# Last tokens of two attentions in four column groups, a scan for a suffix sum, and fewer value tiles in a chain of two transformer blocks

## The reference

```python
xn = rms_norm(h, norm_gains[layer, 0])
proj = xn @ w_in[layer]
q_a, k_a, v_a, f_a, q_b, k_b, v_b, g_a, g_b = split(proj)
# forgetting attention, 8 heads of 64, s <= t
s = q_a k_a / 8 + c[t] - c[s]        # c = cumsum(log sigmoid(f_a + b))
o_a = softmax(s) v_a
# stick-breaking attention, 8 heads of 64, s < t
z = q_b k_b / 8
log_keep = log_sigmoid(-z)
later = cumsum(log_keep, reverse) - log_keep
o_b = exp(log_sigmoid(z) + later) v_b
mixed = (sigmoid(g_a) * (o_a @ w_o_fox) + sigmoid(g_b) * (o_b @ w_o_sb)) @ w_out
# end of block 2
h = h + sigmoid(hn @ ple_w_gate) * (p @ ple_w_proj)
out = rms_norm(h, final_norm)
```

## Time and profile before

| | |
|---|---|
| median of 3 runs | 2233.86 us (2232.55 to 2235.23) |
| profiled execution, own time | 2239.25 us |
| profiled execution, span | 2237.4 us |
| mean granted TensorE clock | .989 of full speed |
| busy: PE, DVE, ACT, POOL | 98%, 44%, 33%, 45% |
| chain that ended last | PE 79%, issue 8%, DVE 7%, POOL 4%, ACT 2% |
| DMA | 194.93 MB, mean 87 GB/s |

### The profile page before, as it was taken

One profiled execution on the slowest core, in us unless ns is written; L12 is line 12 of the kernel. 1 busy time (PEld: TensorE's weight loads), 2 busy tenths in 40 slices (PEclk: granted clock), 3 DMA queues, 4 the chain that ended last, 5 costly groups with the idle time before them and its releaser, 6 DMA issues.

```text
span 2237.4 us, 31159 instructions
## 1 busy us (share of the span) xinstructions
PE 2197.2 (98%) x12456; PEld 1888.3 (84%) x12456; DVE 983.5 (44%) x1432; ACT 736.1 (33%) x971; POOL 1001.2 (45%) x800
## 2 busy tenths in 40 slices
PE   8999999989999999999999999999999999999998
PEld 7897988989999887888888887878777888888886
DVE  5134233458988505422200718751776442322027
ACT  4133243432222215322211414553336332222133
POOL 4322211555555547555544544154431554555442
PEclk9999999999999999999999999999999999999998
DMA  4311111222222222422222221013220223222231
GB/s 160 100 63 58 62 47 38 95 76 76 94 94 94 103 94 76 150 94 94 94 96 101 89 107 66 20 62 119 103 94 20 76 94 108 95 97 94 94 118 70
DMA packets 31837, 194.93 MB, mean 87 GB/s; under 512 B 3968, under 2 KB 4480, under 8 KB 9984
## 3 DMA queue, kind: packets, MB, share of 16 engines
q1 hardware_dynamic: 26352, 182.66, 22.9%
q10 hardware_dynamic: 5392, 10.94, 1.5%
HBM read 189.23 MB, written 4.23 MB: 86 GB/s over the span
## 4 chain that ended last, share of the span: by engine, by line
PE 79%; issue 8%; DVE 7%; POOL 4%; ACT 2%; DMA 0%; SPq 0%; DVEq 0%; POOLq 0%; ACTq 0%
PE ps L2104 69%; POOL wlo L617 4%; PE ps L2628 2%; DVE sqa L1365 1%; PE ps L2376 1%; PE ps L2836 1%; PE ps L2753 1%; PE ps L2810 1%; DVE x2lo L1353 1%; PE ps L2726 1%; PE ps L2359 1%; ACT whi L682 0%; PE ps L2791 0%; PE ps L2416 0%; DVE sd L1929 0%
## 5 line engine op out<-in xcount | busy, mean ns | idle before, releaser
L617 POOL TENSOR_TENSOR wlo<-raw,whi 128x512 fp32r<-128x512 f32 (+2 forms) x796 | 1001.0, 1289 | 1207.4 <-ACT whi L682 1117.1
L682 ACT CAST whi<-raw 128x2048 fp32r<-128x2048 f32 x165 | 315.3, 1911 | 826.2 <-PE ps L2104 767.5
L2104 PE MATMUL ps<-x2hi,whi 128*128 128x512 f32 x1136 | 451.3, 397 | 2.3 <-POOL wlo L617 1.2
L2104 PE MATMUL ps<-x2hi,wlo 128*128 128x512 f32 x1136 | 443.3, 390 | 0.0
L2104 PE MATMUL ps<-x2lo,whi 128*128 128x512 f32 x1136 | 443.1, 390 | 0.0
L2104 PE MATMUL ps<-xhi,whi 128*128 128x256 f32 x1344 | 277.9, 289 | 19.0 <-DVE xlo L1418 9.6
L2104 PE MATMUL ps<-xlo,whi 128*128 128x256 f32 x1344 | 274.2, 286 | 0.0
L2104 PE MATMUL ps<-xhi,wlo 128*128 128x256 f32 x1344 | 274.0, 286 | 0.0
L2104 PEld LDWEIGHTS ps<-x2hi,whi 128*128 128x128 f32 x1136 | 214.1, 188 | 52.5 <-issue 7.8
L2104 PEld LDWEIGHTS ps<-x2lo,whi 128*128 128x128 f32 x1136 | 214.0, 188 | 45.3 <-issue 2.6
L2104 PEld LDWEIGHTS ps<-x2hi,wlo 128*128 128x128 f32 x1136 | 213.8, 188 | 44.9
(11 more groups left out here) (399 smaller groups left out, 2779.8 us busy)
## 6 DMA issues: line engine op xcount, KB each, us to landing
raw<-wstream SPq DMA_DIRECT2D x170, 1024.0 KB, 4.8
h<-h SPq DMA_DIRECT2D x4, 528.0 KB, 8.6
ncb<-c_rows ACTq DMA_DIRECT2D x8, 256.0 KB, 3.6
ple_rows<-ple_out ACTq DMA_DIRECT2D x4, 512.0 KB, 4.0
bias<-bias_rows ACTq DMA_DIRECT2D x8, 256.0 KB, 4.5
ple<-ple_rows ACTq DMA_DIRECT2D x4, 512.0 KB, 5.4
out_dram<-outb SPq DMA_DIRECT2D x8, 256.0 KB, 2.9
raw<-wstream ACTq DMA_DIRECT2D x4, 256.0 KB, 7.3
```

The lines of the kernel that those rows point to most:

```text
L617: return nc.gpsimd.tensor_tensor(wlo[b][:, cols], raw[b][:, cols], whi[b][:, cols].bitcast(F32), ALU.subtract)
L682: nc.scalar.copy(whi[b][:], raw[b][:]).then_inc(sig("hi_done"), 1)
L2104: ins = mm(dst, w[slot][:, cols], xx(tok), start=first and p_ == 0, stop=last and p_ == 2, skip_group_check=True)
```

## The change

It does six things.

- The probabilities' turn and the output of both corners are in four column groups (`turn_corner`, `corner_out`): five products per group with the values as the moving side, 128 columns, query-major in 32 rows; `corner_back` turns the 128x128 result after a copy by ScalarE two steps on.
- The stick-breaking corner's scores are query-major in four groups like the fox's. Its suffix sum is a `tensor_tensor_scan` of VectorE backwards over the keys, with ScalarE's exp, ln and exp around it; masks come from a small tile loaded with `fw0`.
- The fifth value tile has, in place of eight k-steps of three matmuls, two calls of `v_tail` (`rows_at` lists j = 4 only for k = 3 and 7): eight matmuls each, the last 32 tokens' activations in float32 (`x_tail`, made by VectorE) with `whi` and with `wlo` in four groups, a k-step each. The four groups' sums stay apart in the fifth block of 128 rows, and the corner's last turned block repeats its 32 keys four times, so that the output's product adds them. `rcol` gets its fifth column from a copy of `rt` repeated four times.
- `V_ORDER` so has 34 items and `T_GATES` and `T_END` are 98 and 226; `tiles_by(step)` is max(8 x step - 6, 5 x step), so steps 0 and 1 have five tiles and all others of fox eight, of which a QKB chunk's last is the sixth.
- Which chunks VectorE evacuates and which units ScalarE casts in a step follows from `tiles_by`, so both shift.
- At the end of block 2 ScalarE scales the result of seven of the eight chunks, the last weight unit is cast one gate earlier, its low parts come in pieces of 128 columns that TensorE waits for quarter by quarter, and the turns are in another order.

The diff, cut to its core:

```diff
@@ -436,18 +442,19 @@
-        V_FIRST = [(j, k) for js in ((0, 1, 2), (3, 4)) for half in range(2) for j in js
-                   for k in range(4 * half, 4 * half + 4)]
-        V_ORDER = [(j, k) for half in range(2) for j in (0, 1) for k in range(4 * half, 4 * half + 4)]
-        V_ORDER += [(2, k) for k in range(KC)]
-        V_ORDER += [(j, k) for half in range(2) for j in (3, 4) for k in range(4 * half, 4 * half + 4)]
+        def rows_at(js):
+
+            return [(j, k) for half in range(2) for j in js for k in range(4 * half, 4 * half + 4) if j < 4 or k % 4 == 3]
+
+        V_FIRST = rows_at((0, 1, 2)) + rows_at((3, 4))
+        V_ORDER = rows_at((0, 1)) + rows_at((2,)) + rows_at((3, 4))
...
-            return min(KC * step, T_END)
+            return min(max(KC * step - 6, 5 * step), T_END)
...
@@ -814,6 +835,9 @@
+                if n == 2:
+                    act.wait_ge(sig("o_done"), 1)
+                    nc.scalar.copy(fox_pt[1][:, 0:P], o_bank(0)[:, 2 * P:3 * P]).then_inc(sig("fox_pt"), 1)
...
@@ -862,21 +886,30 @@
+                if n == 2:
+                    act.wait_ge(sig("o_done"), O_SB + 1)
+                    nc.scalar.copy(sb_a[1][:, P:2 * P], o_bank(0)[:, 2 * P:3 * P]).then_inc(sig("sb_a"), 1)
...
-                    w = sb_width(n)
-                    for x in range(2):
+                    for x in range(2 if n else 1):
...
-                        logs = sb_l[x][:, 0:w]
+                        logs = sb_l[x][:, 0:sb_width(n)] if n else corner_l[:]
...
+                if n == 0:
+                    act.wait_ge(sig("sb_sp"), 1)
+                    nc.scalar.activation(corner_p[:], corner_p[:], ACT.Exp).then_inc(sig("sb_a"), 1)
...
-                if m >= 0:
+                if m == 0:
+                    act.wait_ge(sig("sb_acc"), 1)
+                    nc.scalar.copy(sb_a[0][:, 0:3 * P], bank(4)[:, 0:3 * P])
+                    nc.scalar.copy(sb_a[0][0:OLD, 3 * P:4 * P], bank(4)[0:OLD, 3 * P:4 * P])
+                    nc.scalar.copy(sb_a[1][:, 0:P], bank(5)[:, 0:P]).then_inc(sig("sb_a"), 1)
+                elif m > 0:
...
-                        if m >= 1:
-                            act.wait_ge(sig("o_done"), NF + m)
+                        act.wait_ge(sig("o_done"), O_SB + m + 1)
...
@@ -1280,14 +1313,22 @@
+            def scale_out(k):
+
+                nc.scalar.activation(fin[:, k, :], hview(k), ACT.Copy, scale=cv[:, G_FIN + k:G_FIN + k + 1]
+                                     ).then_inc(sig("fin_ready"), 1)
+
...
-                if i == 1:
+                gate(i, slice(2 * i, 2 * i + 2))
+                if i == 0:
...
-                gate(i, slice(2 * i, 2 * i + 2))
...
+                scale_out(2 * i)
+                scale_out(2 * i + 1)
...
+            scale_out(6)
...
@@ -1435,6 +1476,12 @@
+            gains = cv[:, G_PRE:G_PRE + KC].rearrange("p (k a) -> p k a", a=1).to_broadcast([P, KC, 32])
+            step.up(vec.tensor_tensor(x_tail[:], h[:, :, TAIL], gains, ALU.mult))
+            step.wait()
+            vec.tensor_copy(one_a[0:1, 0:P].rearrange("p (a c) -> p a c", c=32),
+                            rt[0:1, TAIL].rearrange("p (a c) -> p a c", a=1).to_broadcast([1, 4, 32])
+                            ).then_inc(sig("rt_ready"), 1)
...
@@ -1582,11 +1629,24 @@
-            dve.wait_ge(sig("o_done"), NF)
+            dve.wait_ge(sig("o_done"), O_SB)
...
-                if n < NS:
+                if n == 0:
+                    z = ps[:, 4 * BANK:4 * BANK + T1]
+                    dve.wait_ge(sig("sb_z"), 1)
+                    vec.tensor_scalar(corner_l[:].bitcast(I32), z.bitcast(I32), -2 ** 31, None, ALU.bitwise_or
+                                      ).then_inc(sig("sb_abs"), 1)
+                    dve.wait_ge(sig("sb_l"), 1)
+                    step.up(vec.scalar_tensor_tensor(out=corner_p[:], in0=z, scalar=0.0, in1=corner_l[:], op0=ALU.max,
+                                                     op1=ALU.add))
+                    step.wait()
+                    step.up(vec.tensor_tensor_scan(corner_l[:], one_col.to_broadcast([P, T1]), corner_p[:, T1 - 1::-1],
+                                                   0.0, ALU.mult, ALU.add))
+                    step.wait()
+                    vec.tensor_tensor(corner_p[:], z, corner_l[:, T1 - 1::-1], ALU.subtract).then_inc(sig("sb_sp"), 1)
+                elif n < NS:
...
@@ -2053,8 +2113,10 @@
-                for k in chunks:
-                    dve.wait_ge(sig("ple_added"), k + 1)
+                if chunks == (KC - 1,):
+                    k = KC - 1
+                    dve.wait_ge(sig("ple_added"), KC)
+                    dve.wait_ge(sig("fin_ready"), k)
...
@@ -2179,6 +2241,15 @@
+
+            def v_tail(u0, half, banks):
+
+                for p_, ww in enumerate((whi, wlo)):
+                    for g in range(4):
+                        ins = mm(bank(banks[0])[group(g)], x_tail[:, 4 * half + g, :],
+                                 ww[(u0 + half) % 2][:, g * BANK:(g + 1) * BANK].bitcast(F32),
+                                 start=(half == 0 and p_ == 0), stop=(half == 1 and p_ == 1), skip_group_check=True)
+                return ins
...
@@ -2229,9 +2301,9 @@
-                if k == 0:
+                if k == (0 if j < 4 else 3):
...
-                ins = v_tile(u0, j, k, STAGE1[d])
+                ins = v_tile(u0, j, k, STAGE1[d]) if j < 4 else v_tail(u0, k // 4, STAGE1[d])
...
@@ -2257,7 +2329,31 @@
-            pe.wait_ge(sig("exact_r"), 4)
+            def turn_corner(p_, low, high):
+
+                for b in range(3):
+                    nc.tensor.transpose(low[:, b * P:(b + 1) * P], p_[:, b * P:(b + 1) * P], ident[:])
+                nc.tensor.transpose(low[0:OLD, 3 * P:4 * P], p_[:, 3 * P:3 * P + OLD], ident[:])
+                for g in range(4):
+                    ins = mm(high[group(g), 0:P], p_[:, TAIL], ident[:], start=True, stop=True, skip_group_check=True)
+                return ins
+
+            def corner_out(low, high, v):
+
+                dst = o_bank(0)[:, 2 * P:3 * P]
+                for b in range(5):
+                    src = high[:, 0:P] if b == 4 else low[:, b * P:(b + 1) * P]
+                    rows = slice(0, OLD if b == 3 else P)
+                    for c in range(4):
+                        ins = mm(dst[group(c)], src[rows, group(c)], v[rows, b, c * P:(c + 1) * P], start=(b == 0),
+                                 stop=(b == 4), skip_group_check=True)
+                ins.then_inc(sig("o_done"), 1)
+
+            def corner_back(src):
+
+                nc.tensor.transpose(o_bank(0)[:, 0:P], src, ident[:]).then_inc(sig("o_done"), 1)
+
+            pe.wait_ge(sig("exact_r"), 5)
...
@@ -2297,20 +2393,12 @@
-                    pe.wait_ge(sig("fox_pt"), fox_item(m, 1))
+                    pe.wait_ge(sig("fox_pt"), fox_copied(m, 1))
...
-                        for c in range(4):
-                            vc, qc = slice(c * P, (c + 1) * P), slice(32 * c, 32 * c + 32)
-                            for b in range(3):
-                                mm(dst[:, qc], vf[:, b, vc], fox_pt[0][:, b * P + 32 * c:b * P + 32 * c + 32],
-                                   start=(b == 0 and c == 0), stop=False, skip_group_check=True)
-                            mm(dst[:, qc], vf[0:META, 3, vc], fox_pt[0][0:META, 3 * P + 32 * c:3 * P + 32 * c + 32],
-                               start=False, stop=False, skip_group_check=True)
-                            ins = mm(dst[:, qc], vf[:, 4, vc], fox_p4[:, qc], start=False, stop=(c == 3),
-                                     skip_group_check=True)
+                        corner_out(fox_pt[0], fox_p4, vf)
...
@@ -2335,21 +2423,18 @@
-                        pe.wait_ge(sig("sb_a"), sb_item(n - 2, 1))
+                        pe.wait_ge(sig("sb_a"), sb_used(n - 2, 1))
...
-                        pe.wait_ge(sig("fox_pt"), fox_item(NF - 1, 1))
+                        pe.wait_ge(sig("fox_pt"), fox_copied(NF - 1, 1))
...
-                        for x in range(2):
-                            for b in range(5):
-                                s0 = b * P if b < 4 else T1 - P
-                                for cc in range(2):
-                                    c = 2 * x + cc
-                                    mm(zs[x][:, b * 64 + 32 * cc:b * 64 + 32 * cc + 32], qkb[:, 4 + c, s0:s0 + P],
-                                       qz[:, c, :], start=(b == 0 and cc == 0), stop=False, skip_group_check=True)
-                            every = madds_tail.rearrange("p (a c) -> p a c", a=1).to_broadcast([P, 4, META])
-                            mm(zs[x][:, 256:320].rearrange("p (a c) -> p a c", c=META), ident_r[:], every, start=False,
-                               stop=False, skip_group_check=True).then_inc(sig("sb_z"), 1)
+                        z = ps[:, 4 * BANK:4 * BANK + T1]
+                        for a, e in ((0, SEQ), (SEQ, T1)):
+                            for c in range(4):
```

(19 more changed lines are left out.)

101 lines of the change are left out of this document (54 added, 47 removed).

## The result

| | before | changed |
|---|---|---|
| median of 5 runs | 2235.23 us (2232.55 to 2237.24) | 2250.20 us (2245.80 to 2253.16) |
| profiled execution, own time | 2239.25 us | 2250.20 us |
| its span | 2237.4 us | 2248.3 us |

The account below looks back on a forecast made before the run. TensorE, busy 98% of the span, was taken as the bound. Gains of 26.4 against 28.8 of waits and 5.5 of clock gave +7.9, say 8.0: 2247.3 us profiled, less 5.4 for the median, 2241.9; range 2229 to 2252.

Parts of the forecast that it names:

- the likeliest case: The forecast itself for the whole kernel: 2241.9 us, own range 2238 to 2248, chance .62.
- V tail: Fifth value tile: four calls gain 3.2, less .8 for low parts and .4 for VectorE's new operations; gain 2.0 us.
- Fox corner: Fox attention's corner: output 7.42 us becomes 1.3, and 2.6 of low clock behind it goes; gain 8.3 us.
- Stick-breaking corner: That attention's corner: shorter scores and output, VectorE's scan hidden beside dense tiles, less low clock; gain 13.8 us.
- End: Tail of the kernel: two pairs of scalings and one more leave VectorE for ScalarE; gain 2.3 us.
- Waits for VectorE: Chunks beginning within steps 1 to 8: TensorE waits .97 in five, 2.6 in two and 3.5 in step 5.
- Waits for low parts: Steps 9 and 13: TensorE waits for low parts of weights cast in the same step, 4.8 and 9.2 us.
- Clock in the gaps: Low clock after waits in steps 3, 5, 7, 9 and 13: 5.5 us more, ends 0 and 13.
- The turn from the profile to the median: Whole kernel: 2247.3 us forecast for the profiled execution, lowered by the 5.4 its old profile stood over the median.
- the waits are short: Rival: VectorE comes in time in steps 3, 5, 7 and clock falls in step 13 alone; 2232.8 us, chance .21.
- the weights are there: Rival: no wait in steps 9 and 13, as ScalarE casts early enough; 2224.2 us, faster, chance .14.
- the groups do not run side by side: Rival: column groups in V tail calls, corner outputs and scores run in turn; 28.4 us more, some 2270, chance .03.

Follow-up runs that it names:

- aligned plan: The changed kernel with only its step plan altered, so that every chunk begins with a step again: 2212.96 us, ratio .9892.

## Why the prediction was right or wrong

The direction, the likeliest case and its mechanism were right, and 2250.2 lies in the range. The size was not: 15.0 us in place of 8.0, and above the likeliest case's own 2238 to 2248. Step by step:

- **V tail, -2.0 forecast: -.5 between two groups, not told from nothing.** A call takes 1.85 us (88.66 to 90.51), 1.94 was said, and the low parts ate their .8 (the wait of .33 became 1.16); in the aligned plan they took .9 more in step 13. Wrong was the .4 for VectorE's two operations. They took 1.39 and 1.18 us, and 1.79 of that fell on TensorE. The row of a 256-wide operation that reads PSUM was the wrong neighbour: these two work on SBUF, while GpSimd makes low parts (34.15 to 40.14).
- **Fox corner, -8.3: -7.1 by its own run.** The output is 1.23 us (1.3 said). The 7.42 of the old one was read as work, but 2.0 of it were clock: 5.38 at full clock. So the work gained is some 4.1 and the rest is clock, which differs between executions.
- **Stick-breaking corner, -13.8: some -12.** Scores 1.18, turn .91, output 1.24, where 1.3, .86 and 1.3 stood; the cover over the scan's chain held, by 1.5 us as said (its last exp ends at 286.72, the turn starts at 288.26). The size is a difference of runs: the kernel with the old fox output, 2220.6, against before, 2235.4, is 14.8 for this corner and the end, less 2.7 to 2.9 for the end.
- **End, -2.3: -2.7 by its own run, -4.0 between the profiles.** The mechanism was taken too narrowly: three pairs of scalings on VectorE, not two, stood in the stretch, and VectorE's operations beside GpSimd's wide low parts took 1.64 to 1.78 us each in place of .69.
- **Waits for VectorE, +13.6: +12.5.** The five of .97 were .80 to .89, the two of 2.6 were 2.40 and 2.39, and the 3.5 was 3.39. That the cast makes the three long ones late was shown by changing two calls over.
- **Waits for low parts, +14.0: +14.1.** 5.38 and 9.50 us, less the .46 and .34 that were there before. S+9.88 was right to .1: the reduction starts at 228.88 and TensorE goes on at 238.69.
- **Clock in the gaps, +5.5: +8.7 in the profiled execution.** This is the term of the sum that was too small: 3.0 in step 13 (2.2 forecast), 1.7 in step 9 (1.5), 0 in step 5 (.8), 1.7 and 2.3 in steps 3 and 7 (.5 each). The upper end of 13 holds it, though step 13 passes its own 2.6. These sizes are one draw; with step 12 at tile 93 step 5 had .54 and step 7 had 1.00, behind the same waits.
- **The turn from the profile to the median** is the other step that failed. From profile to profile the change cost 10.9 us and not 15.0, against 8.0 forecast. The profiled execution of before stands 4.0 us over its median (5.4 over that of the three runs shown), and its clock had fallen at the earlier trace rows and in both windows of the earlier trace rows. The executions of the two kernels with only a new end, whose code is the same there, had .73 and .85 in the first window and 1.00 in both others. Over the whole stretches (109.90 to 125.00, 250.00 to 264.10, 275.00 to 290.00) the clock took 10.2 us in before and 5.2 and 3.4 in these two, so before lost 5.0 and 6.8 us more, which is the size of the 4.0 to 5.4. Even there .88 stood over the old stick-breaking scores. Adding up the profile's lost clock (2.6 + 1.3 + 1.5) as gain, and then going down by 5.4 us to the median, counted much of the same loss twice. That this lifted before's profile over its median rests on these few executions, since the others have no trace.

Added up in runs, the changes of the kernel's work give 24 us (ratio .9892 with the aligned plan, forecast 26.4), and the step plan takes 39 by the ratios or 37 by the medians (forecast 34.3).

Of the rivals, *the waits are short* and *the weights are there* fell with the first profile, and *the groups do not run side by side* with the output's 1.23 us. The price of some 62 ns per matmul, which the Trainium skill, TensorE: Matmul & The Clock Gate, in "Wait — 56ns, not 53.3ns?", gives for hardware decode off, is not paid here: forty took 1.23 us, 31 ns each. Which way the decode is set, no run shows.

It stays open how much of the low clock is chance in each place, since no experiment fixed the clock. Of the 36.4 us between the spans of the changed kernel and of the aligned plan, 25.8 are waits and 8.7 clock, less 1.7 for the clock at the aligned plan's start; the other 3.6 are not assigned.

## What to carry to other kernels

When work is taken out of a plan in which several engines share buffers, look at what the shift does to the places where they hand over: here, one tile that ended a unit on the wrong side of a step's boundary cost 11.6 us, and each chunk that began within a step cost .8 to 3.4 us of waiting. All such places together cost more than the work saved. Read for each engine the order of what it issues, and put what others wait for (a copy of 128 columns) ahead of what they need much later (a cast of 2048). A profiled execution is one draw of the clock: compare its own time with the median and find the reason before its slow stretches are counted as gain.
